# Gate/up weights of a mixture of experts: pieces of 16 KB per partition and 2 MB a transfer, or 32 KB and 4 MB

## The reference

```python
h = rms_norm(x, norm2_g[l]) * (1.0 + sc2) + sh2
logits = h @ router_w + router_b            # (256, 32)
top_val, top_idx = top_k(logits, 4); gates = softmax(top_val)
# for every expert e, on the tokens that chose it:
g, u = split(h_e @ w_gu[e] + b_gu[e])       # w_gu[e]: 1024 x 2048, 8 MB
act = (min(g, 7) * sigmoid(1.702 * min(g, 7))) * (clip(u, -7, 7) + 1)
y_e = act @ w_down[e] + b_down[e]           # w_down[e]: 1024 x 1024, 4 MB
x = x + g2 * sum_e gate_e * y_e
return rms_norm(x, final_g)
```

## Time and profile before

| | us |
|---|---|
| median of 3 runs | 1372.68 (1370.77 to 1373.67) |
| the profiled execution's own time | 1371.69 |
| its span, first to last instruction | 1369.7 |
| first part, to the first L1500 | 419.5 |
| 32 items and the end | 950.2 |
| period of an item in the middle (start of its L1500 to the next one's) | 28.15 |

### The profile page before, as it was taken

One profiled execution on the slowest core, in us unless ns is written; L12 is line 12 of the kernel. 1 busy time (PEld: TensorE's weight loads), 2 busy tenths in 40 slices (PEclk: granted clock), 3 DMA queues, 4 the chain that ended last, 5 costly groups with the idle time before them and its releaser, 6 DMA issues.

```text
span 1369.7 us, 16175 instructions
## 1 busy us (share of the span) xinstructions
PE 1298.5 (95%) x5988; PEld 608.3 (44%) x5989; DVE 468.8 (34%) x924; ACT 186.5 (14%) x378; POOL 15.6 (1%) x48
## 2 busy tenths in 40 slices
PE   4999999999999999999999999999999986999996
PEld 2876876778853333333333333333333332333332
DVE  1020766333134332333334342343423332324333
ACT  2101322333011000100001000010001000001001
POOL 0000000110000000000000000000000000000000
PEclk9999999999999999999999999999999999999999
DMA  9746758224668999999999999999999999399993
GB/s 364 255 160 246 246 185 298 103 91 171 263 266 349 406 431 429 429 429 428 428 428 429 428 428 429 388 421 429 428 429 429 429 429 428 151 428 429 428 428 155
DMA packets 55983, 477.55 MB, mean 349 GB/s; under 512 B 4863, under 2 KB 4948, under 8 KB 28308
## 3 DMA queue, kind: packets, MB, share of 16 engines
q1 hardware_dynamic: 55652, 476.11, 84.5%
q10 hardware_dynamic: 304, 1.06, 0.2%
HBM read 476.10 MB, written 1.05 MB: 348 GB/s over the span
## 4 chain that ended last, share of the span: by engine, by line
PE 89%; DMA 7%; ACT 1%; DVE 1%; issue 1%; SPq 0%; DVEq 0%
PE bank L1500 31%; PE bank L1533 16%; PE bank L1204 13%; DMA down_ring<-in_w_down 5%; PE bank L1452 4%; PE bank L1489 4%; PE bank L1322 4%; PE bank L1195 4%; PE bank L1467 3%; PE bank L1385 2%; DMA gu_ring<-in_w_in 2%; PE bank L1461 2%; ACT scratch L657 1%; PE bank L1478 1%; PE bank L1283 1%
## 5 line engine op out<-in xcount | busy, mean ns | idle before, releaser
L1500 PE MATMUL bank<-gu_ring,scratch 128*64 128x512 f32 x2048 | 462.1, 598 | 5.8 <-issue 4.2
L1500 PEld LDWEIGHTS bank<-gu_ring,scratch 128*64 128x64 f32 x2048 | 143.5, 137 | 289.7 <-issue 285.8
L1533 PE MATMUL bank<-down_ring,scratch 128*64 128x512 f32 x1024 | 227.3, 596 | 1.9 <-DMA down_ring<-in_w_down 1.9
L1204 PE MATMUL bank<-gu_ring 128*128 128x256 f32 x768 | 174.3, 385 | 2.2 <-DMA gu_ring<-in_w_in 2.2
L1204 PEld LDWEIGHTS bank<-gu_ring 128*128 128x128 f32 x768 | 146.1, 193 | 25.4 <-issue 4.7
L1533 PEld LDWEIGHTS bank<-down_ring,scratch 128*64 128x64 f32 x1024 | 70.4, 137 | 134.5 <-issue 126.2
L1024 DVE TENSOR_TENSOR scratch<-bank,bgu 128x512 f32<-128x512 f32 x32 | 22.1, 692 | 280.5 <-PE bank L1467 280.5
L661 ACT ACTIVATE scratch<-bank 128x512 f32<-128x512 f32 x32 | 19.1, 597 | 708.7 <-PE bank L1500 708.7
L1006 DVE TENSOR_TENSOR xres<-xres,bank 128x512 f32<-128x512 f32 x132 | 81.9, 682 | 38.7 <-PE bank L1489 38.7
L1038 DVE TENSOR_TENSOR scratch<-bank,scratch 128x512 f32<-128x512 f32 x32 | 22.1, 692 | 182.0 <-PE bank L1533 182.0
L1452 PE MATMUL bank<-xn,onehot 128*64 128x512 f32 x264 | 71.2, 618 | 0.0
(11 more groups left out here) (258 smaller groups left out, 775.4 us busy)
## 6 DMA issues: line engine op xcount, KB each, us to landing
gu_ring<-in_w_gu SPq DMA_DIRECT2D x128, 2048.0 KB, 21.3
down_ring<-in_w_down SPq DMA_DIRECT2D x64, 2048.0 KB, 14.4
gu_ring<-in_w_in SPq DMA_DIRECT2D x32, 1024.0 KB, 7.9
gu_ring<-in_w_ada SPq DMA_DIRECT2D x20, 1024.0 KB, 7.0
down_ring<-in_w_ada SPq DMA_DIRECT2D x4, 1024.0 KB, 10.3
gu_ring<-in_w_pa SPq DMA_DIRECT2D x4, 1024.0 KB, 6.2
gu_ring<-in_w_pb SPq DMA_DIRECT2D x4, 1024.0 KB, 6.6
gu_ring<-in_w_o SPq DMA_DIRECT2D x4, 1024.0 KB, 10.3
```

The costliest lines, as they stand in the source:

```text
L1204: last = M(dst[:, b * T:(b + 1) * T], group_chunk(group, kt // 4)[:, kt % 4, cols], hT[:, kt, :], start=kt == 0, stop=kt == KT - 1)
L1500: last = M(bank[f // 2][64 * a:64 * a + 64, :], xT[:, kt % 4, kt // 4, :], gu_ring[:, 8 * half + kt, f * 512:(f + 1) * 512], start=kt == 0 ...
L1533: last = M(bank[7][64 * a:64 * a + 64, :], act_sb[:, kt % 4, kt // 4, :], down_ring[:, kt // 2, (kt % 2) * D + a * 512:(kt % 2) * D + (a + ...
```

## The change

A gate/up transfer now takes 512 rows of w_gu, four adjacent rows to a partition: 32 KB in one piece, 4 MB a transfer, two transfers for an item, each into four slots. It waits until PE has used the four k-tiles that stood in them, and PE waits for it before kt = 0 and kt = 4. Items 0 and 1 still come by 2 MB, now as two of the four rows (16 KB out of each 32 KB). The waits of PE before kt = 2 and kt = 6 stay in the program, with a constant that is only of use for items 0 and 1. The row order goes by fours in the second norm, its modulation, the router and the gathering.

```diff
-            def load_gu(expert, half, j):
-                first = 8 * half + 2 * j
-                sp.dma_start(gu_ring[:, first:first + 2, :].rearrange("p r n -> p (r n)"),
-                             w_gu[0, bass.ds(expert, 1), j * 2 * P:(j + 1) * 2 * P, :]
-                             .rearrange("a (p r) n -> p (a r n)", r=2)).then_inc(slot_in[first], 16)
+            def load_gu(expert, half, j, rows_=4, of=0):
+                first = 8 * half + 4 * j + of
+                sp.dma_start(gu_ring[:, first:first + rows_, :],
+                             w_gu[0, bass.ds(expert, 1), j * 4 * P:(j + 1) * 4 * P, :]
+                             .rearrange("a (p r) n -> p (a r) n", r=4)[:, of:of + rows_, :]).then_inc(slot_in[first], 16)
+
+            def load_gu_pair(expert, half, pair):
+                load_gu(expert, half, pair // 2, 2, 2 * (pair % 2))
...
-                for j in range(4):
-                    sp.wait_ge(gu_used, item * 8 + (2 * j - 14))
+                for j in range(2):
+                    sp.wait_ge(gu_used, item * 8 + (4 * j - 12))
                     load_gu(item, half, j)
...
-            act.dma_start(vt_pairs[0:4, :], norm2_g[0, :].rearrange("(r f) -> r f", f=2 * P)).then_inc(pairs_in, 16)
+            act.dma_start(vt_fours[0:2, :], norm2_g[0, :].rearrange("(r f) -> r f", f=4 * P)).then_inc(fours_in, 16)
...
-            for r in range(2):
-                last = nc.tensor.transpose(bank[5][:, 12 * r:12 * r + 12], vt_pairs[:, r:2 * P:2], ident[0:12, 0:12])
+            for r in range(4):
+                last = nc.tensor.transpose(bank[5][:, 6 * r:6 * r + 6], vt_fours[:, r:4 * P:4], ident[0:6, 0:6])
...
-                transposes_by_pairs(6, x_raw).then_inc(takenT_done, 1)
+                transposes_by_fours(6, x_raw).then_inc(takenT_done, 1)
...
                 for kt in range(KT):
-                    if kt % 2 == 0:
+                    if kt % 4 == 0:
                         pe.wait_ge(slot_in[8 * half + kt], fills * 16 + 16 * USES[8 * half + kt])
+                    elif kt % 2 == 0:
+                        pe.wait_ge(slot_in[8 * half + kt], 16 + 16 * USES[8 * half + kt])
...
                     for q in range(4):
+                        pair = xn[:, tt, q // 2 * 512:(q // 2 + 1) * 512].rearrange("t (p r) -> t r p", r=4)
                         last = M(bank[4][FCAP * q:FCAP * (q + 1), 0:2 * P], onehot[:, tt, 0:FCAP],
-                                 xn[:, tt, q * 2 * P:(q + 1) * 2 * P], start=tt == 0, stop=tt == TT - 1,
+                                 pair[:, 2 * (q % 2):2 * (q % 2) + 2, :], start=tt == 0, stop=tt == TT - 1,
```

More of the change, by code:

```diff
@@ L197, in build @@
         small_in = sem("small_in")
[L198 removed]
+        fours_in = sem("fours_in")
         bgu_in = sem("bgu_in")
@@ L715, in _ @@
             V.tensor_scalar(nsub[:], vec[:, R_SUB:R_SUB + 1], 1.0 - LAM_INIT, None, ALU.mult).then_inc(vec_ready, 1)
[L717 to L721, removed]
+            dve.wait_ge(foursT_done, 1)
+            by_fours = bank[5][:, 0:24].rearrange("p (r n) -> p r n", r=4)
+            V.tensor_copy(vec[:, R_N2:R_N2 + KT].rearrange("p (j r) -> p r j", r=4), by_fours[:, :, 0:2])
+            own.then(V.tensor_copy(vec[:, R_ADA + M_SH2:R_ADA + M_G2].rearrange("p (j r) -> p r j", r=4),
+                                   by_fours[:, :, 2:6]))
             V.tensor_copy(c_cols, vec[:, R_C:R_C + KT].unsqueeze(2).to_broadcast([P, KT, 32])).then_inc(vec_ready, 1)
@@ L1122, in _ @@
             nc.tensor.transpose(bank[7][:, 0:R_END], vt, ident[0:R_END, 0:R_END]).then_inc(vecT_done, 1)
[L1123 to L1126 removed]
+            pe.wait_ge(fours_in, 32)
+            for r in range(4):
+                last = nc.tensor.transpose(bank[5][:, 6 * r:6 * r + 6], vt_fours[:, r:4 * P:4], ident[0:6, 0:6])
+            last.then_inc(foursT_done, 1)
             pe.wait_ge(vec_ready, 2)
@@ L1162, in ada_columns @@
                 for q in (0, 2):
-                    in_pairs = 4 * part_ + q in (M_SH2 // 4, M_SC2 // 4)
+                    by_four = 4 * part_ + q in (M_SH2 // 4, M_SC2 // 4)
                     for blk in range(4):
                         cols = slice(16 * part_ + 4 * q + blk, 16 * part_ + 4 * q + blk + 5, 4)
-                        first = 2 * P * (blk // 2) + blk % 2
-                        block_rows = rows[part_][:, first:first + 2 * P - 1:2] if in_pairs else rows[part_][:, blk * P:(blk + 1) * P]
+                        block_rows = rows[part_][:, blk:4 * P:4] if by_four else rows[part_][:, blk * P:(blk + 1) * P]
                         last = M(bank[7][:, cols], block_rows, first_of[:, q:q + 2], start=True, stop=True)
@@ L1393, in transpose_x1 @@
                 for n in range(4):
-                    first = half * 512 + (n // 2) * 2 * P + n % 2
                     last = nc.tensor.transpose(bank[b + half][:, n * P:(n + 1) * P],
-                                               xres[:, tt, first:first + 2 * P - 1:2], ident[:])
+                                               xres[:, tt, half * 512 + n:(half + 1) * 512:4], ident[:])
                 last.then_inc(xT_done, 1)
@@ L1455, in take @@
                     last.then_inc(taken_done, 1)
-            def transposes_by_pairs(b, src):
-                for j in range(4):
-                    first = (j // 2) * 2 * P + j % 2
-                    last = nc.tensor.transpose(bank[b][:, j * P:(j + 1) * P], src[:, first:first + 2 * P - 1:2], ident[:])
-                return last
             def transposes_by_fours(b, src):
@@ L1556, in further @@
                 for c in range(2):
-                    last = nc.tensor.transpose(bank[6][:, c * P:(c + 1) * P], x_raw[:, c:2 * P:2], ident[:])
+                    last = nc.tensor.transpose(bank[6][:, c * P:(c + 1) * P], x_raw[:, c * P:(c + 1) * P], ident[:])
                 last.then_inc(f_takenT, 1)
```

24 lines of the change are left out of this document (11 added, 13 removed).

## The result

| | median | runs | ratio to before, 95% interval |
|---|---|---|---|
| before | 1371.55 us | 6 (1369.76 to 1373.67) | |
| after | 1380.17 us | 6 (1376.09 to 1382.02) | 1.0052 [1.0039, 1.0066] |

The change makes the kernel slower by 0.5%, 7 to 9 us. The forecast of 1372.6 missed it, and so did its range, by 2.7 us. The profiled execution of after took 1380.27 us.

What follows compares the result with a forecast made beforehand. The prediction took PE to bound the kernel, except for DMA in two short places, 3.9 us together. Its terms summed as 1371.69 + 1.2 - 1.3 + 0 = 1371.6 us profiled, median 1372.6, range 1369.8 to 1377.5.

Steps and rivals of the forecast that it cites:

- What bounds the kernel: Whole kernel: PE bounds it, except DMA in two short places (items 14 and 15, further pass), 3.9 us together.
- Term 1: Item 2's first gate/up load is issued 5.5 us later; DMA's lead shrinks by 3.0 us, bounds 2.8 and 5.5.
- Term 2: Gate/up loads in 32 KB pieces save 0.14 us of DMA time an item, bounds 0 and 0.29.
- Terms 1 and 2 up to item 16: Waits up to item 16 grow from 2.4 to 3.6 us, so +1.2 us.
- no saving: Rival: larger pieces save nothing per piece on DMA; 1375.7 us, chance 0.15.
- the idle stretch in full: Rival: DMA's idle time at item 2 counts 5.5 us instead of 3.0; 1375.1 us, chance 0.09.
- slower: Rival: 32 KB pieces might run 1% slower on DMA, 0.2 us an item; 1380.0 us, chance 0.07.
- faster: Rival: DMA saves more per item and all waits go; 1368.8 us, chance 0.06.
- Term 4: Row order by fours in weight loads and the further pass's gather costs nothing; the gather bounded at 0 to 1.1 us.
- Term 3: PE waits for 4 MB; further pass ends 1.3 us earlier, with the 1.48 us down-load wait at 1147.72.
- the clock: Rival: half clock after the further pass may vanish (-2.4 us) or lengthen as much; 1370.2 to 1375.0, chance 0.11.

Runs made afterwards that it cites:

- e9: The kernel before, unchanged, profiled a second time; 1372.06 us.
- e7: e3 with the first half of an item's gate/up weights as two early 2 MB loads, the second as one of 4 MB; 1374.84 us, 1.0013.
- e8: e7 with the order of loads changed at item 15 instead of 17; 1374.89 us, 1.0012.
- e2: The changed kernel with its late issue, but each 4 MB transfer as two of 2 MB (16 KB pieces); 1382.85 us, 1.0072.
- e1: The changed kernel's row order by fours, with the 2 MB loads and waits of before; 1375.27 us, 1.0028.
- e12: The kernel before, with only the modulation columns' weight loads reading every fourth column; tokens go elsewhere, no further pass; 1347.65 us.
- e10: The changed kernel, unchanged, profiled a second time; 1378.77 us, 1.0042.
- e3: The changed kernel, with ScalarE reordering the modulation rows on the copy out of PSUM, so PE loads adjacent columns; 1376.65 us, 1.0031.
- e5: e3 with the second 4 MB of item 2's gate/up weights issued only after k-tile 1 of item 1; 1385.51 us, 1.0093.
- e6: The kernel before, with the order of loads (down ahead of next gate/up) changed at item 15 instead of 17; 1371.38 us, 0.9996.
- e11: The kernel before, with only the further pass's gather reading every fourth column of xn; 1372.41 us, 1.0002.
- e4: The kernel before in its row order, with only the changed 4 MB transfers and their waits; 1378.41 us, 1.0037.

## Why the prediction was wrong

**What was right.** *What bounds the kernel* held inside the loop: the changed kernel loses and gains nothing in items 2 to 11, 16 to 23 and 26 to 31. *Term 1*: 3.0 us of lead lost, measured 2.9, and 2.2 against e9's lead. *Term 2*: 0.14 us an item saved, measured 0.15: the lead shrinks by 1.06 an item in all kernels with 4 MB loads throughout, by 1.21 with 2 MB and by 1.14 in e7 and e8, which have one of each. e2, which has term 1 without term 2, is 2 to 3 us slower than the changed kernel. *Terms 1 and 2 up to item 16*: +1.2 forecast, +0.9 between the first pair of profiles, nothing between the second. The rivals on DMA (no saving, the idle stretch in full, slower, faster) are all out. That the slower one named 1380.0, next to the measured 1380.17, is luck: the rate in the loop is 430 GB/s, and the time was lost elsewhere.

**The step that failed: Term 4.** It said "reading every second column takes 208 ns and every fourth 209" and "nothing", and for the moving operand "since the weight loads show no step from two to four I take 0". The rows behind both the earlier trace rows were loads of transposes. The change also moves the loads of the modulation columns, ordinary products with every second column as weights, at 194 ns on average; with every fourth they take 327, and the step costs 1.75 us with no cover. What stands behind them costs as much again: 3.4 us of half clock, 1.7 us of time, at 178 to 180 us in all five profiles with these loads (after, e1, e2, e12, and e10 with 6.8 us more), and in none of the nine others. e1, e3 and e12 show it from three sides: 3 us of the loss. Why the clock falls there, with PE busy, no run shows. The prediction had these loads under "the row order", at the price of another kind of load.

The same step's moving operand was bounded at 0 to +1.1 and taken at 0; it is +0.92, in nine profiles 1.99 to 2.02. The Trainium skill (SBUF — State Buffer, section Door 1: The DMA port swizzle), which says that every new 16-byte line pays and that two hits in a line are needed for full speed, was right in both places: two float32 of a line at a step of two, one at a step of four. It doesn't tell why the transposes' loads show no such step, 208 and 209 ns.

**The step that was missing: the first pass through the loop's code.** Term 1 replayed which data would be in the queue when (counted from item 0, its landings come within 1 us of the measured ones), and saw a dry spell at 446 to 447 only as DMA time. It didn't ask who else uses these engines. The instruction fetch does. Measured: 26.0 us after item 0 with an empty queue (e5), 26.1 to 26.7 in before, e6, e9, e11 and e12, 27.5 in e1, 28.3 in e2, 28.4 to 29.4 with 4 MB transfers. PE's loss in items 0 and 1 goes with it: 0.8 us in e1, 1.7 to 2.8 in e2 and with 4 MB, and 1.7 more in the two profiles (after and e3) whose stall was 3.3 us or longer and was followed by half clock. Why e10's fetch was 0.8 us earlier than after's isn't settled. In e1, with the loads of before, the last gate/up load of item 2 lands 27.3 us after item 0, in before 26.5, and the fetch starts 0.2 us behind it in both; in e9 it starts 0.9 us ahead of it, so that landing alone doesn't set it.

**Term 3** forecast -1.3 for the further pass. Its DMA part came true: the second half of item 25's down weights lands 47.6 and 47.9 us after item 24's start in the changed kernel (47.4 in e3, 47.6 in e4; 48.5 in e5, which waits for gate/up weights at item 24), against 48.9 in before and e9, so 1.1 to 1.3 earlier (e1, e2 and e11, with 2 MB loads, have 48.3 to 49.1). That the wait of 1.48 is gone doesn't show it, for the kernel before has none either in its second profile, e9:

```profile
1147.27 3.64 PE L1577 MATMUL bank<-down_ring,scratch 128*32 128x512 f32 x32 [2.72 <-DVE scratch L1079]
```

The forecast took a wait for granted that comes only when PE is early enough. What was won went to the gather's 0.9 and to *the clock*, which was among the rivals with the right mechanism and at the right place; how much each took can't be told apart. The two other stretches of half clock, at 178 and at 454.7, were in no rival. Half clock between 1120 and 1180 us, and the time of items 24 and 25, in thirteen profiles:

| half clock, us | items 24 and 25, us |
|---|---|
| 6.8 | 90.0 (before), 88.7 (e3) |
| 10.2 | 90.0 (e9), 90.4 (e1), 90.9 (e5), 91.8 (e8) |
| 13.6 | 91.0 (after), 91.0 (e10) |
| 17 | 92.2 (e7), 92.7 (e6), 93.1 (e11), 93.5 (e2) |
| 23.9 | 94.3 (e4) |

Taken over all kernels, that is about 0.3 us for each microsecond of half clock, waits of up to 1.5 us for weights included. Some of it falls where PE would wait anyway: e9 has 2.4 us more in the gate/up products of the further pass and no wait for down, and ends within 0.3 of before. How much half clock a run gets isn't a property of the kernel alone (6.8 us in before, 10.2 in e9); whether the change makes it likelier stays open.

**The account.** Over two pairs of profiles the loss is 2.5 and 6.8 ahead of the loop (1.75 and 2.1 of it the loads, the rest clock, that near 30 us included), 4.2 and 1.9 in items 0 and 1, 0.9 and 0 at the down loads, 1.0 and 1.0 in the further pass: 8.6 and 9.7, where the spans differ by 8.6 and 9.6. The range failed because its upper bounds were bounds on DMA's work in the queue, and neither of the two largest causes is one.

## What to carry to other kernels

When a change alters a stride, list every instruction whose operand gets it and look up each kind by itself, weights of ordinary products and of transposes and moving operands apart. When a change puts more data in the queue ahead of the first run of a branch or loop half, expect the code's own fetch behind it; a queue that is dry at that moment may be worth more than the DMA time it wastes. A wait that you take away returns if the next place that needs the same queue is short of data as well: e6 moved 2.4 us of waits and e8 part of e7's 2.1, and neither won anything.

## What was not expected of the hardware

Float32 weight loads of 128x128: 194 ns on average where eight of sixteen read every second column, 309 to 332 for every fourth in ordinary products, but 208 and 209 for both in transposes. A moving operand of 128x256 float32 with every fourth column takes nearly twice the time, 2.01 against 1.07 us for 16 products. Instruction fetches of 16 KB use the same DMA engines as the data and start up to 3.4 us late when 4 MB or more are queued (e3 against e5); PE goes on 1.3 to 1.6 us after the fetch's packet ends. 32 KB pieces run at 430 GB/s in the loop, as this window of after shows (510 to 550 us, against 428 in the earlier trace rows):

```profile
DMA packets 823, 17.19 MB, mean 430 GB/s; under 512 B 95, under 2 KB 95, under 8 KB 95
```
